# Cross-attention of a float32 decoder trunk: v as the stationary operand, probabilities scaled before they are transposed, head outputs cast straight from PSUM

## The reference

```python
q = (h @ wq).reshape(bsz, s, N_XATTN_HEADS, XATTN_HEAD_DIM)
k, v = jnp.split(m @ wkv, 2, axis=-1)
scores = jnp.einsum("bshd,bmhd->bhsm", q, k).astype(jnp.float32) / math.sqrt(XATTN_HEAD_DIM)
p = jax.nn.softmax(scores, axis=-1).astype(v.dtype)
o = jnp.einsum("bhsm,bmhd->bshd", p, v).reshape(bsz, s, D_MODEL)
return o @ wo
```

## Time and profile before

| | |
|---|---|
| median of 3 runs | 1151.02 us |
| profiled execution | 1151.14 us |
| its span, first to last instruction | 1149.4 us |
| PE busy | 1126.4 us (98%) |
| DVE busy | 676.4 us (59%) |
| ACT busy | 549.1 us (48%) |
| granted TensorE clock, mean | 0.995 of full |

### The profile page before, as it was taken

How to read it: one execution, slowest core, us unless ns; L and a number is a source line. 1 busy time by engine, 2 the same in 40 slices (tenths; PEclk the granted TensorE clock), 3 DMA queues, 4 the chain that set the end, 5 groups by cost and what they waited for, 6 DMA issues and landing times.

```text
span 1149.4 us, 12931 instructions
## 1 busy us (share of the span) xinstructions
PE 1126.4 (98%) x5194; PEld 930.8 (81%) x5194; DVE 676.4 (59%) x751; ACT 549.1 (48%) x615; POOL 24.5 (2%) x23
## 2 busy tenths in 40 slices
PE   6999999999999999999999999999999999999997
PEld 4888888888888888888888888888888888888885
DVE  5555545699754555554565555458996446555542
ACT  4544434654555454443354444347464555444441
POOL 1000000000000000000000000000000000000000
PEclk8999999999999999999999999999999999999999
DMA  9655554653552466555476654565455345655451
GB/s 287 206 183 170 181 191 152 231 177 127 204 177 95 148 184 187 183 194 185 151 230 185 185 183 166 183 201 183 147 182 171 139 131 183 183 183 183 165 187 70
DMA packets 159260, 202.69 MB, mean 176 GB/s; under 512 B 6922, under 2 KB 115030, under 8 KB 159200
## 3 DMA queue, kind: packets, MB, share of 16 engines
q1 hardware_dynamic: 158112, 200.82, 53.6%
q10 hardware_dynamic: 1088, 1.05, 0.3%
HBM read 200.79 MB, written 1.05 MB: 176 GB/s over the span
## 4 chain that ended last, share of the span: by engine, by line
PE 76%; issue 16%; DVE 4%; ACT 3%; DMA 0%; POOL 0%; DVEq 0%; POOLq 0%; SPq 0%; ACTq 0%
PE acc L1214 23%; PE acc L1216 23%; PE acc L1215 22%; PE turn L1138 4%; DVE w_lo L727 2%; ACT w_hi L393 1%; PE acc L1385 1%; PE acc L1408 1%; DVE arena L910 1%; DMA xs<-in_x 0%; PE acc L1312 0%; PE acc L1188 0%; POOL rstd L368 0%; PE acc L1189 0%; DVE xg L752 0%
## 5 line engine op out<-in xcount | busy, mean ns | idle before, releaser
L727 DVE TENSOR_TENSOR w_lo<-w_raw,w_hi 128x2048 fp32r<-128x2048 f32 x191 | 428.2, 2247 | 262.6 <-ACT w_hi L393 262.6
L393 ACT CAST w_hi<-w_raw 128x2048 fp32r<-128x2048 f32 x191 | 357.3, 1871 | 132.7 <-PE acc L1216 122.8
L1214 PE MATMUL acc<-w_hi,xT_hi 128*128 128x512 f32 x888 | 353.5, 398 | 5.6 <-DVE w_lo L727 5.6
L1216 PE MATMUL acc<-w_hi,xT_lo 128*128 128x512 f32 x888 | 347.3, 391 | 0.0
L1215 PE MATMUL acc<-w_lo,xT_hi 128*128 128x512 f32 x888 | 346.3, 390 | 0.0
L1214 PE MATMUL acc<-w_hi,hT_hi 128*128 128x512 f32 x608 | 240.9, 396 | 0.8 <-DVE hT_lo L895 0.8
L1216 PE MATMUL acc<-w_hi,hT_lo 128*128 128x512 f32 x608 | 237.2, 390 | 0.0
L1215 PE MATMUL acc<-w_lo,hT_hi 128*128 128x512 f32 x608 | 236.7, 389 | 0.0
L1214 PEld LDWEIGHTS acc<-w_hi,xT_hi 128*128 128x128 f32 x888 | 167.3, 188 | 38.1 <-DVE w_lo L727 5.8
L1216 PEld LDWEIGHTS acc<-w_hi,xT_lo 128*128 128x128 f32 x888 | 167.1, 188 | 36.1
L1215 PEld LDWEIGHTS acc<-w_lo,xT_hi 128*128 128x128 f32 x888 | 167.5, 189 | 33.0
(11 more groups left out here) (107 smaller groups left out, 479.0 us busy)
## 6 DMA issues: line engine op xcount, KB each, us to landing
w_raw<-in_ffn_w_in SPq DMA_DIRECT2D x174, 512.0 KB, 4.9
w_raw<-in_ffn_w_out SPq DMA_DIRECT2D x80, 512.0 KB, 4.4
w_raw<-in_mix_w_in SPq DMA_DIRECT2D x32, 512.0 KB, 4.5
w_raw<-in_xattn_wkv SPq DMA_DIRECT2D x32, 512.0 KB, 4.3
w_raw<-in_mix_w_out SPq DMA_DIRECT2D x16, 512.0 KB, 4.3
w_raw<-in_xattn_wq SPq DMA_DIRECT2D x16, 512.0 KB, 4.5
w_raw<-in_xattn_wo SPq DMA_DIRECT2D x16, 512.0 KB, 4.2
w_raw<-in_ffn_w_out SPq DMA_DIRECT2D x16, 256.0 KB, 2.8
```

The lines of the kernel that those rows point to most:

```text
L393: act.copy(w_hi[:, u % SLOTS, 0:n], w_raw[:, u % SLOTS, 0:n]).then_inc(w_split_hi, 1)
L727: dve.tensor_tensor(w_lo[:, u % SLOTS, 0:n], w_raw[:, u % SLOTS, 0:n], w_hi[:, u % SLOTS, 0:n].bitcast(F32), ALU.subtract).then_inc(w_spli ...
L1214: pe.matmul(o, hi, wh, start=(first and j == 0), stop=False)
L1216: ins = pe.matmul(o, lo, wh, start=False, stop=(last and j == nk - 1))
```

## The change

The product of a head is turned round. v is now the stationary operand (128 columns of it at a time) and the transposed probabilities the moving one, so that the result has the channels on the partitions, which is the layout that the output projection reads. The four turns o0 to o3 of each layer are gone, with `attn_out` and the buffer `attn`. Since the rows of x are now the columns of the result, the division by the row sum can't be a scale for each partition there; it is done before the probabilities are transposed, by DVE: `normalise` has the reciprocal, and then two multiplications of 128x256 for a head, in place. The probability turns wait for `pnorm_ready` in place of `probs_ready`. ACT casts the hi part from the accumulator, and DVE subtracts from there.

The places of the work change as well. Both turns of q of heads 2 and 3 stand between the tiles of U_V1. Products 0 and 1 and the turns p2 and p3 stand between the tiles of U_V1+1, products 2 and 3 between the tiles of U_WO. ACT evacuates the first tile of v's second half, casts heads 0 and 1, and then evacuates the second tile. DVE's lo parts of heads 0 and 1 stand before its copies of p2 and p3.

```diff
-                + ["p0", "p1", "p2", "p3", "o0", "o1", "o2", "o3"]
+                + ["p0", "p1", "p2", "p3"]
...
-                values(1)
+
+                def attn_hi(h):
+                    act.wait_ge(pv_done, at.at(HEADS, h + 1))
+                    act.copy(hT_hi[:, Y_KT + 2 * h:Y_KT + 2 * h + 2, :],
+                             acc[OPAIR[h // 2]][h % 2][:, :].rearrange("p (k s) -> p k s", k=2)).then_inc(oT_hi_ready, 1)
+
+                values(1, [0])
+                attn_hi(0)
+                attn_hi(1)
+                values(1, [1])
                 weights_to(U_WO + 2, at)
-
-                def attn_out(h):
...
-                attn_out(0)
-                attn_out(1)
-                attn_hi(0)
-                attn_out(2)
-                attn_hi(1)
-                attn_out(3)
                 attn_hi(2)
                 attn_hi(3)
...
-                def inv_sum(h):
+                def normalise(h):
                     dve.wait_ge(probs_ready, at.at(HEADS * T, T * (h + 1)))
-                    dve.reciprocal(rinv[:, h, :], psum_rows[:, h, :]).then_inc(rinv_ready, 1)
+                    steps.link(dve.reciprocal(rinv[:, h, :], psum_rows[:, h, :]))
+                    for t in range(T):
+                        ins = dve.tensor_scalar(probs[:, T * h + t, :], probs[:, T * h + t, :], rinv[:, h, t:t + 1], None, ALU.mult)
+                    ins.then_inc(pnorm_ready, 1)
...
-                inv_sum(2)
-                inv_sum(3)
+                normalise(2)
+                normalise(3)
+                weights_to(U_WO + 1, at)
+                attn_lo(0)
+                attn_lo(1)
                 probs_turn(2)
                 probs_turn(3)
                 weights_to(U_WO + 2, at)
-                for h in range(HEADS):
-                    attn_lo(h)
+                attn_lo(2)
+                attn_lo(3)
...
-                unit(U_V1, at, VPAIR[1], hT_hi, hT_lo, MEM_KT, True, False, between=lambda t: query_turn(1, t))
+                unit(U_V1, at, VPAIR[1], hT_hi, hT_lo, MEM_KT, True, False,
+                     between=lambda t: None if t else (query_turn(1, 0), query_turn(1, 1)))
...
                     pe.wait_ge(pT_ready, at.at(HEADS, h + 1))
-                    for t in range(T):
+                    for d in range(2):
                         for m in range(2):
-                            ins = pe.matmul(acc[OPAIR[h // 2]][h % 2][:, t * S:(t + 1) * S], pT[h][:, m, t * P:(t + 1) * P],
-                                            v_half[h // 2][:, m, (h % 2) * HD:(h % 2 + 1) * HD], start=(m == 0), stop=(m == 1))
+                            col = (h % 2) * HD + d * P
+                            ins = pe.matmul(acc[OPAIR[h // 2]][h % 2][:, d * S:(d + 1) * S], v_half[h // 2][:, m, col:col + P],
+                                            pT[h][:, m, :], start=(m == 0), stop=(m == 1))
                     ins.then_inc(pv_done, 1)
...
+                def first_heads():
+                    pe.wait_ge(v_ready, at.at(4, 2))
+                    pv(0)
+                    pv(1)
+                    probs_turns(2)
+                    probs_turns(3)
+
+                def last_heads():
+                    pe.wait_ge(v_ready, at.at(4, 4))
+                    pv(2)
+                    pv(3)
 
                 probs_turns(0)
                 probs_turns(1)
...
+                unit(U_V1 + 1, at, VPAIR[1], hT_hi, hT_lo, MEM_KT + GK, False, True, between=lambda t: None if t else first_heads())
                 pe.wait_ge(oT_ready, at.at(HEADS, 2))
-                unit(U_WO, at, WO_PAIR[0], hT_hi, hT_lo, Y_KT, True, False, between=lambda t: None if t else attn_turns(3))
+                unit(U_WO, at, WO_PAIR[0], hT_hi, hT_lo, Y_KT, True, False, between=lambda t: None if t else last_heads())
```

## The result

The changed kernel takes 1144.94 us, the median of five runs (1144.14 to 1145.36), against 1151.40 us for the kernel before in five runs (1150.92 to 1151.91). The ratio is 0.9946, with a 95% interval of 0.9934 to 0.9959. The forecast was 1145.3, in a range of 1144.2 to 1147.6. The profiled execution took 1144.94 us with a span of 1143.2, against 1151.14 and 1149.4: 6.20 us less.

The account below looks back on a forecast made before the run. PE (TensorE), busy 98% of the span, was taken as the bound. 0.93 + 1.90 = 2.83 us a layer, 2.87 by the rebuilt stretch, taken as 2.85, so 5.7 for two layers: 1145.3 us, range 1144.2 to 1147.6.

Parts of the forecast that it names:

- the stretch: PE time from the scores of head 0 to the start of U_WO+1: 35.76 us before, 32.9 forecast.
- The wait before the scores of head 2: PE idles 0.67 us for ACT's copy of a q turn; with restart, 0.93 us a layer would go.
- The turns o0 to o3: Four turns on PE in each layer; removing them would save their places, 1.90 us a layer.
- The exchanged operands: Products on PE with v as weights would keep their pace, 1.72 us a head.
- all six waits: PE's waits at p0/p1, product 0, p2/p3, U_WO, products 2/3 and U_WO+1; each claimed at least 1.1 us of cover.
- DVE's multiplication: Scaling of a head's probabilities on DVE: two multiplications, 0.82 us a head, hidden from PE.
- Rival A: Cover before product 0 or U_WO+1 partly missing, DVE's chain being longer: about 1147 us, chance 0.10.
- Rival B: Each removed PE turn saves its whole duration, 0.60 us, not its place: 1144.4 us, chance 0.07.
- C: No change: PE reaches weights that are not ready and waits there instead; near 1151 us, chance 0.03.
- D: Slower: late weights of U_WO+2 hold up ACT's casts, PE waits before U_WO+1; landing at 374 gives 1154; chance 0.02.

Follow-up runs that it names:

- The q turns alone: Kernel before with only the q turns of heads 2 and 3 moved between the tiles of U_V1: ratio 0.9984, median 1149.06 us.
- the doubled turns: Changed kernel with each of the turns p0 to p3 done twice into the same bank: ratio 0.9975, median 1148.01 us.
- two delays: Changed kernel, DVE scaling heads 2 and 3 before copying p0 and p1: 1145.65 us; changed kernel, four idle DVE subtractions before the copy of p0: 1146.47 us.
- in a lump: Changed kernel with products 0 and 1, p2 and p3, products 2 and 3 together between U_V1+1 and U_WO: ratio 0.9977, median 1148.15 us.
- ACT's order as it was: Changed kernel with ACT evacuating both tiles of v's second half ahead of the casts of heads 0 and 1: ratio 1.0010, median 1152.31 us.
- the two with edits of the mixers: Changed kernel with the am turn between the tiles of U_MI+5: 1143.77 us; the same plus U_MO+1's blocks reordered, its wait mid-tile: 1141.36 us.

## Why the prediction was right

The mechanism, the places and the sum held. That the time came within 0.4 us of the forecast is in part luck, since executions of one kernel lie up to 2.3 us apart (1149.68 to 1152.01 for the kernel before) and the sum didn't have the pause of DVE; the stretch, forecast at 32.9 and measured at 32.89, is what bears the sum out.

- The wait before the scores of head 2, with its restart: 0.93 us a layer forecast. The q turns alone gave 0.92, and taking them back from the changed kernel cost 0.93.
- The turns o0 to o3: 1.90 forecast, 1.94 measured (35.76 - 33.82). The price of a turn by itself, 0.44, came out of the doubled turns. The figure of about 275 ns for one transpose (the Trainium skill, TensorE: Matmul & The Clock Gate, Part 4: PE-mode transpose), which the page gives as a duration in one kernel and for bf16, isn't the price of one in a stream here, in float32: 16 more cost 1.76 us a layer, so 0.11 each.
- The exchanged operands: a product keeps its pace. A pair takes 3.45 us (359.46 to 362.91), as two of 1.72 did.
- The cover: all six waits stayed out of PE's list. The one at product 0 was tested with two delays and is 1.8 us, where the expectation of the delay had 1.9. The others are read from the trace and weren't tested one by one.
- DVE's multiplication was mis-sized, without effect, since it is hidden. I set 0.41 us each by the nearest row; two take 0.62 from start to end, in a group mean of 351 ns.
- Rival A (lost cover) cost nothing in the changed kernel. What it describes is real: it is 0.19 us a layer when DVE scales first, 1.43 in a lump, and 2.87 to 4.46 with ACT's order as it was. Rival B (durations, not places) is out by the doubled turns, C by the stretch itself. D didn't occur; it named ACT's order as the place from which a loss could come, with late weights as the cause. The order that loses is another (the evacuation of v ahead of the casts), which I hadn't listed.
- What the sum didn't have is the 0.35 us of DVE's pause in the second layer. It is most of why the profiled execution gained 6.20 and not 5.75. The medians of 1151.40 and 1144.94 are 6.46 apart, with an interval (4.7 to 7.6) that holds both.

## What to carry to other kernels

On an engine that is busy for 98%, an edit is worth the difference of start times that it takes away, wait and restart included; build the new stretch up from those differences and put each wait of the bounding engine on that clock, with the work of the other engines in order. The q turns and the heads add up (0.92 and 1.94), but within the heads removing work isn't enough: without the placing of what is left it is worth 0.5 of the 1.94. The placing is lost when one in-order engine keeps its old order: here the moved evacuation on ACT decided over more than the whole gain. An instruction of another kind (a transpose, a small product) goes between two tiles of a long unit, with the tile behind it as cover for whoever reads its result.

## What the runs showed that I had not expected

An idle time of 2.58 us on PE, in the same execution, was followed by 1.2 GHz in the first layer and not in the second. Its price was 4.46 or 2.87 us.

What differs between executions lies at the start. The scores of head 0 in the first layer started between 341.2 and 343.5 us in the eleven traces that have no edit ahead of them. Set against the changed kernel matmul by matmul, these, and the two with edits of the mixers but for those edits, differ up to there by more than some 0.2 us at two places only: in the first unit, near 14 us, by -1.0 to +0.4 us, and near 27 us by -0.5 to +0.2. The first unit of the kernel before, whose matmuls are at the slower pace until past 12.7:

```profile
11.86 0.63 PE L1188 MATMUL acc<-w_hi,xT_hi 128*128 128x512 f32 x1
12.29 0.63 PE L1189 MATMUL acc<-w_hi,xT_lo 128*128 128x512 f32 x1
12.71 1.75 PE L1195 MATMUL acc<-w_lo,xT_hi 128*128 128x512 f32 x4
```

and that of the kernel with doubled turns, where matmuls are at the faster pace already from 12.29 on:

```profile
11.93 0.52 PE L1179 MATMUL acc<-w_hi,xT_hi 128*128 128x512 f32 x1
12.29 0.39 PE L1180 MATMUL acc<-w_hi,xT_lo 128*128 128x512 f32 x1
12.51 1.09 PE L1186 MATMUL acc<-w_lo,xT_hi 128*128 128x512 f32 x4
```

At the second place the granted clock says the same. From 26.0 to 27.6 us it is 0.50 of full, the level of 1.2 GHz, in the kernel before, and 1.00 in the one with doubled turns (third from the end, in this order):

```profile
26.00:27.60 1.60, 1.60 (x5) 1.30 (x4) 1.41 (x1) 0.16 (x1) 0.68 (x1) 0.50 1.09 350
26.00:27.60 1.60, 1.60 (x9) 1.29 (x8) 1.60 (x1) 0.00 (x0) 0.00 (x0) 1.00 1.03 358
```

So the matmuls reach the full clock earlier or later. That is where the single runs of one kernel may get their spread of about 2 us from; the traces show it for one execution of each kernel, not for the spread itself. A stretch inside the program is free of it and agrees to 0.04 us between layers and executions of kernels that have the same stretch, so it tells apart what medians don't.
